# Feed-forward weight sums: two of the four by adding transfers, two on GpSimd, lower block row negated

## The reference, cut to what matters

```
def _swiglu(x, w_gate, w_up, w_down):
    return (jax.nn.silu(x @ w_gate) * (x @ w_up)) @ w_down
```

## Time and profile before

| | us |
|---|---|
| median of 3 runs | 2102.5 (2102.32 to 2103.25) |
| span of the profiled execution | 2102.9 |
| PE busy | 2066.9, 98% of the span |
| DVE busy | 1351.0, 64% |
| ACT busy | 1013.6, 48% |
| POOL busy | 722.4, 34% |

### The profile page before, as it was taken

One profiled execution on the slowest core, in us unless ns is written; L12 is line 12 of the kernel. 1 busy time (PEld: TensorE's weight loads), 2 busy tenths in 40 slices (PEclk: granted clock), 3 DMA queues, 4 the chain that ended last, 5 costly groups with the idle time before them and its releaser, 6 DMA issues.

```text
span 2102.9 us, 31133 instructions
## 1 busy us (share of the span) xinstructions
PE 2066.9 (98%) x10658; PEld 1753.4 (83%) x10658; DVE 1351.0 (64%) x2278; ACT 1013.6 (48%) x1788; POOL 722.4 (34%) x544
## 2 busy tenths in 40 slices
PE   8999999999999999999999999999999999999998
PEld 6778888888988888988887788888878888888886
DVE  6497863667752366674277889899767337676523
ACT  4466663533433353434344577767655325344322
POOL 2133452513233163442337511211165315233331
PEclk9999999999999999999999999999999999999999
DMA  5333263334433244443335322222364534445331
GB/s 175 96 103 103 76 225 100 119 117 155 140 123 97 80 130 130 150 149 110 91 94 171 100 71 89 73 80 86 118 203 131 178 97 126 135 132 167 100 99 61
DMA packets 74383, 251.31 MB, mean 120 GB/s; under 512 B 8264, under 2 KB 8520, under 8 KB 73776
## 3 DMA queue, kind: packets, MB, share of 16 engines
q1 hardware_dynamic: 51120, 182.08, 28.2%
q0 software_dynamic: 11456, 40.72, 5.8%
q10 hardware_dynamic: 11712, 27.27, 3.5%
HBM read 229.57 MB, written 18.89 MB: 118 GB/s over the span
## 4 chain that ended last, share of the span: by engine, by line
PE 87%; DVE 8%; ACT 2%; issue 2%; DMA 1%; DVEq 0%; SPq 0%; ACTq 0%
PE bank L188 25%; PE bank L190 25%; PE bank L189 25%; PE bank L195 3%; PE bank L194 3%; PE bank L2166 1%; DVE w_lo L162 1%; DMA w_raw<-stream 1%; PE bank L2833 1%; PE bank L920 1%; PE bank L2835 1%; PE bank L347 1%; PE bank L349 1%; PE bank L354 1%; PE bank L2841 1%
## 5 line engine op out<-in xcount | busy, mean ns | idle before, releaser
L162 DVE TENSOR_TENSOR w_lo<-w_raw,w_hi 128x1024 fp32r<-128x1024 f32 x337 | 454.0, 1350 | 410.2 <-ACT w_hi L157 407.0
L188 PE MATMUL bank<-xn_hi,w_hi 128*128 128x512 f32 (+1 forms) x1432 | 554.5, 387 | 6.1 <-DVE w_lo L162 4.2
L157 ACT ACTIVATE w_hi<-w_raw 128x1024 fp32r<-128x1024 f32 x337 | 354.7, 1055 | 417.7 <-PE bank L190 249.6
L189 PE MATMUL bank<-xn_lo,w_hi 128*128 128x512 f32 (+1 forms) x1432 | 538.6, 376 | 0.0
L190 PE MATMUL bank<-xn_hi,w_lo 128*128 128x512 f32 (+1 forms) x1432 | 538.5, 376 | 0.0
L188 PEld LDWEIGHTS bank<-xn_hi,w_hi 128*128 128x128 f32 x1432 | 270.2, 189 | 58.0 <-DVE h L622 6.0
L190 PEld LDWEIGHTS bank<-xn_hi,w_lo 128*128 128x128 f32 x1432 | 269.5, 188 | 50.1
L189 PEld LDWEIGHTS bank<-xn_lo,w_hi 128*128 128x128 f32 x1432 | 270.3, 189 | 44.6 <-issue 2.6
L188 PE MATMUL bank<-down_hi,w_hi 128*128 128x512 f32 x528 | 205.8, 390 | 0.0
L190 PE MATMUL bank<-down_hi,w_lo 128*128 128x512 f32 x528 | 205.4, 389 | 0.0
L189 PE MATMUL bank<-down_lo,w_hi 128*128 128x512 f32 x528 | 205.4, 389 | 0.0
(11 more groups left out here) (473 smaller groups left out, 4228.1 us busy)
## 6 DMA issues: line engine op xcount, KB each, us to landing
w_raw<-stream SPq DMA_DIRECT2D x337, 512.0 KB, 3.6
s_raw<-stream POOLq DMA_DIRECT2D x48, 512.0 KB, 6.4
spill_g<-gate_out ACTq DMA_DIRECT2D x16, 256.0 KB, 2.0
m_more<-spill_g POOLq DMA_DIRECT2D x3, 1024.0 KB, 13.2
x<-xt SPq DMA_DIRECT2D x4, 512.0 KB, 6.9
x<-xt ACTq DMA_DIRECT2D x1, 2048.0 KB, 11.5
spill_x<-x ACTq DMA_DIRECT2D x1, 2048.0 KB, 7.6
spill_ga<-ga_out ACTq DMA_DIRECT2D x8, 256.0 KB, 3.3
```

The lines of the kernel that those rows point to most:

```text
L157: nc.scalar.activation(w_hi[:, slot, :], w_raw[:, slot % 2, :], ACT.Copy).then_inc(split_hi, 1)
L162: nc.vector.tensor_tensor(w_lo[:, slot, :], w_raw[:, slot % 2, :], w_hi[:, slot, :], ALU.subtract).then_inc(split_lo, 1)
L188: nc.tensor.matmul(to, a_hi, b_hi, start=start, stop=False, skip_group_check=True)
L189: nc.tensor.matmul(to, a_hi, b_lo, start=False, stop=False, skip_group_check=True)
```

## The change

The lower block row (up) enters the form with its sign turned, so that all four weight sums become additions. S1 and S3 are then made by transfers from DRAM that add into `s_raw` as they land: the first half of the up chunk is added to a22, and the first half of the gate chunk to a21. Both are issued by POOL once the two plain loads have landed, and POOL waits for both of them before it makes S2 and S4 as before. ACT waits for S1 and S3 on the transfers' own semaphores and for S2 and S4 on the count of POOL's sums. The turned sign is taken back in T1, T2 and T4 (a factor of -1 in ACT's `t_high` and DVE's `t_low`) and in the `gated` of the first tile; for this `gated` and `t_low` become scalar_tensor_tensor in place of tensor_tensor, all of them. POOL's loop over bodies is written out in Python, and `square_added`, which only f1 has, gets one more wait on its own last sum.

```
-            for k, n in (("sum", 4), ("hi", 4), ("lo", 4), ("gate", KT), ("gated", 0)):
-                merges[k] += n + 4 * BODIES
+                merges[k] += n + (2 if k == "sum" else 4) * BODIES
...
-                gates_n[g] += 16 * BODIES
+                gates_n[g] += 32 * BODIES
+            def landed(i, g, n):
+                return 32 * i + (gates_loaded[g] - 32 * FIRST_BODY + 16 * n)
...
-                    nc.scalar.activation(t_hi[:, n], t_raw[:, n], ACT.Copy).then_inc(c["hi"], 1)
+                    nc.scalar.activation(t_hi[:, n], t_raw[:, n], ACT.Identity, scale=T_SIGN[n]).then_inc(c["hi"], 1)
...
                 def s_high(n, i):
-                    act.wait_ge(c["sum"], summed(i))
+                    if n in (S1, S3):
+                        act.wait_ge(gates_in[0 if n == S1 else 1], landed(i, 0 if n == S1 else 1, 2))
+                    else:
+                        act.wait_ge(c["sum"], summed(i, 1 if n == S2 else 2))
...
-                    nc.vector.tensor_tensor(to, silu[t][:], to, ALU.mult).then_inc(s["product"], 1)
+                    nc.vector.scalar_tensor_tensor(to, silu[t][:], sign, to, ALU.mult, ALU.mult).then_inc(s["product"], 1)
...
                 def sums(i):
-                    for g in range(2):
-                        pool.wait_ge(gates_in[g], 16 * i + (gates_loaded[g] + 16 * (1 - FIRST_BODY)))
                     a11, a12, a21, a22 = (s_raw[:, g, half, :] for g in range(2) for half in range(2))
-                    nc.gpsimd.tensor_tensor(a22, a21, a22, ALU.add).then_inc(c["sum"], 1)
-                    nc.gpsimd.tensor_tensor(a21, a11, a21, ALU.subtract).then_inc(c["sum"], 1)
-                    pool.wait_ge(c["sum"], summed(i, 2))
-                    nc.gpsimd.tensor_tensor(a11, a22, a11, ALU.subtract).then_inc(c["sum"], 1)
-                    pool.wait_ge(c["sum"], summed(i, 3))
-                    nc.gpsimd.tensor_tensor(a12, a12, a11, ALU.subtract).then_inc(c["sum"], 1)
+                    gate_11, up_21 = (stream[4 * i + (first_in + g)][:, 0:HT * P] for g in range(2))
+                    pool.wait_ge(gates_in[0], landed(i, 0, 1))
+                    pool.wait_ge(gates_in[1], landed(i, 1, 1))
+                    pool.dma_start(a22, up_21, accum_op=ALU.add).then_inc(gates_in[0], 16)
+                    pool.dma_start(a21, gate_11, accum_op=ALU.add).then_inc(gates_in[1], 16)
+                    pool.wait_ge(gates_in[0], landed(i, 0, 2))
+                    pool.wait_ge(gates_in[1], landed(i, 1, 2))
+                    nc.gpsimd.tensor_tensor(a11, a22, a11, ALU.add).then_inc(c["sum"], 1)
+                    pool.wait_ge(c["sum"], summed(i, 1))
+                    nc.gpsimd.tensor_tensor(a12, a12, a11, ALU.add).then_inc(c["sum"], 1)
```

More of the change, by code:

```diff
@@ L279, in build_program @@
         S_AT = ((0, 0), (1, 1), (1, 0), (0, 1))
+        T_SIGN = (-1.0, 1.0, -1.0, -1.0)
         assert BODIES == KT
@@ L298, in feed_forward, with summed @@
             for g in range(2):
-                gates_n[g] += 16 * BODIES
-            def summed(i, n=4):
-                return 4 * i + (c0["sum"] + 4 - 4 * FIRST_BODY + n)
+                gates_n[g] += 32 * BODIES
+            def landed(i, g, n):
+                return 32 * i + (gates_loaded[g] - 32 * FIRST_BODY + 16 * n)
+            def summed(i, n):
+                return 2 * i + (c0["sum"] + 4 - 2 * FIRST_BODY + n)
             def part_made(k, i, n):
@@ L617, in normed, with gated @@
                     nc.vector.tensor_tensor(to, banks[bank][:], norm_r[:], ALU.mult).then_inc(s["scaled"], 1)
-                def gated(to, t, scaled, silus):
+                def gated(to, t, scaled, silus, sign=1.0):
                     dve.wait_ge(s["scaled"], scaled)
                     dve.wait_ge(s["silu"], silus)
-                    nc.vector.tensor_tensor(to, silu[t][:], to, ALU.mult).then_inc(s["product"], 1)
+                    nc.vector.scalar_tensor_tensor(to, silu[t][:], sign, to, ALU.mult, ALU.mult).then_inc(s["product"], 1)
                 def t_low(n):
                     dve.wait_ge(c["hi"], c0["hi"] + n + 1)
-                    nc.vector.tensor_tensor(t_lo[:, n], t_raw[:, n], t_hi[:, n], ALU.subtract).then_inc(c["lo"], 1)
+                    nc.vector.scalar_tensor_tensor(t_lo[:, n], t_raw[:, n], T_SIGN[n], t_hi[:, n], ALU.mult, ALU.subtract
+                                                   ).then_inc(c["lo"], 1)
                 def s_low(n, i):
@@ L675, in dve_part @@
                     nc.vector.tensor_tensor(h_tile(i, 0), h_tile(i, 0), norm_r[:], ALU.mult).then_inc(s["scaled"], 1)
-                    gated(h_tile(i, 0), 0, 4 * i + (2 * b + 3), 2 * i + (b + 2))
+                    gated(h_tile(i, 0), 0, 4 * i + (2 * b + 3), 2 * i + (b + 2), -1.0)
                     finished(dve, first_in, 3, i, N_IN)
@@ L764, in square_added @@
                     nc.gpsimd.tensor_tensor(fin_r[:], fin_r[:], joint_sq[:], ALU.add).then_inc(f["added"], 1)
+                    pool.wait_ge(f["added"], n + 1)
                 pool.wait_ge(c["gate"], c0["gate"] + KT)
@@ L780, in pool_part @@
                     nc.gpsimd.tensor_tensor(fin_r[:], x[:, 0, :], x[:, 0, :], ALU.mult).then_inc(f["added"], 1)
-                    with pool.Fori(FIRST_BODY, FIRST_BODY + KT - 1) as i:
+                    for i in range(FIRST_BODY, FIRST_BODY + KT - 1):
                         next_raw(i)
@@ L785, in pool_part @@
                 else:
-                    with pool.Fori(FIRST_BODY, FT // 2 - 1) as i:
+                    for i in range(FIRST_BODY, FT // 2 - 1):
                         next_raw(i)
```

## The result

The changed kernel takes 2114.9 us (median of 4 runs, 2113.4 to 2115.8), before 2102.9: a ratio of 1.005, interval 1.0038 to 1.0062. It is slower by 8 to 13 us. The profiled execution has a span of 2111.2 against 2102.9. A run's time is 2.0 to 2.6 us over its span wherever both are known. So the profiled execution of after, 2113.4, is the fastest of its four, and that of before, whose time is not known, would have taken about 2105, more than any of its four. The two traces therefore show 8.3 of the 12 us. It also means that the span before should not have been held against the median, as the table of times before does with "within 0.4 us" and the prediction's sum with its 0.4.

A forecast was written before the change was run, and what follows sets the result against it. PE, busy 98% of the 2102.9 us span, was taken as the bound. 2102.9 - 4.2 (removed sums) + 3.9 (`w_lo` stalls) + 0.1 (sign) = 2102.7, or 2102.3 against the median; range 2098.0 to 2118.0.

The forecast's parts named there:

- the loop of `s_raw` closes: Rival, 0.20: the single buffer's chain from issue to issue outlasts a body, from L = 7.3; 2124 at the upper bound.
- loads, issue to landed: First stretch of the `s_raw` chain, the plain loads' landing: 5.8 or 7.9 us, read from two bodies.
- L: Time from the first adding transfer's issue until both have landed: 5.5 us taken, bounds 4.6 to 8.6.
- ACT and DVE up to the next issue: End of the `s_raw` chain: two pairs of `s_hi` and `s_lo`, a copy and a `w_lo`, some 4 us.
- u: Time in us within a body, counted from its first matmul on PE.
- The ceiling: Most that could be gained: 4.2 us (0.20%) that PE loses in 21 bodies against 21.02 us each.
- The removed part: Two of POOL's four sums gone and the sums' place freed beside DVE's chain to L622: -4.2 us.
- POOL's loop written out: Loop over bodies unrolled on POOL; said to fall in POOL's idle time of 4.6 us or more: 0.
- The stall at S2 past s = 3.7: ACT's first `s_hi` waits for POOL's first sum; s up to 3.7 is covered, never reached with L = 5.5: 0.
- s: Start of POOL's first sum in us, counted from the start of the body using it; forecast -0.9 to +1.3.
- The window of s from 0 to 1.1 for `w_lo`: POOL's sums delay DVE's `w_lo` of chunk 2, stalling PE by s in a third of 21 bodies: +3.9 us.
- Sign, longer forms, extra wait: scalar_tensor_tensor on L622 +0.1 us; `t_hi` and `t_lo` in the plain tiles 0; the extra wait of `square_added` 0.

The follow-up runs named there:

- the hold: Kernel with the up chunk first, POOL's two sums of a body also held until DVE has made `w_lo` of chunk 2: 2100.3 us, ratio 0.9982.
- the up chunk first: Changed kernel, but the up chunk is loaded first and both adds are issued when it alone has landed: 2103.6 us, ratio 0.9996.
- the run without adds: Changed kernel with the two adding transfers and their waits left out, nothing in their place: 2101.4 us, ratio 0.9985.

## Why the prediction was wrong

The forecast was no change, 2102.3; the kernel is slower by 12 us, through the mechanism that the prediction has as "the loop of `s_raw` closes", with a chance of 0.20. The measured 2114.9 lies inside the stated range of 2098.0 to 2118.0, but only because that range took in part of this rival. The step that failed is the length of that chain, which was put under a body and is over it: forecast 13.8 + 5.5 = 19.3 us against a body of 21.1, measured 21.9 on average against 21.02. By its terms (medians over the turns inside the loops):

| from issue to issue, us | predicted | measured |
|---|---|---|
| loads, issue to landed | 5.8 or 7.9, mean 6.85 | 8.7 (8.1 to 9.2) |
| L, the adds | 5.5 | 6.4 (5.7 to 6.6; 6.7 to 7.1 in the first turns) |
| two sums | 2.9 | 2.66 |
| ACT and DVE up to the next issue | some 4 | 4.12 |

*The landing of the loads is the step that was off by the most,* 1.9 of the 2.6 us. The two turns that it was read from happen to include nearly the shortest one: over the 21 turns of the trace before, the landing is 5.7 to 8.6, median 7.6, which was there to be read. With the loop written out they are issued 0.4 us earlier and take longer, 8.2 (median of the kernel before with its loop written out). In the changed kernel the first loads inside each loop, at u = 8.6, took 8.7 to 8.9, and the later ones, at 9.6 to 11.8 in the closed chain, 8.1 to 9.2; why they took longer was not tested. With the measured terms the chain closes from L = 5.5 on, not from 7.3, so the L that was forecast would already have stood at the edge, while the measured L of 6.4 in a chain of 13.8 + L would not have closed it.

*L = 5.5 is the second.* It "counted them as copies of 512 KB" and then chose from the low end because the engines are quiet at that time. Measured is 5.7 to 7.1, inside the bounds of 4.6 to 8.6. The quiet did not help: the stretch of the adds shows the engines at 68% for 106 GB/s (the last two columns; the stretch of the copies stands at 37% for 124).

```profile
501.70:508.10 6.40, 6.40 (x47) 6.04 (x46) 2.52 (x3) 0.38 (x1) 1.75 (x2) 1.00 0.68 106
```

Twice the engine time of a copy was the right guess for the movement. Left out was POOL's own issue, 1.8 us for the two together in place of 1.1; the prediction names this as a sign of being wrong. The estimate from the Trainium skill (DMA: Bandwidth & Descriptors, Anatomy of one DMA), 3.8 us, was further off, and this case's runs disagree with it for plain copies too: 4.3 us for two of 256 KB, where by the same reading it gives some 3.2 as an estimate.

*The size of the loss* follows from the chain: 0.85 us a turn over 18 turns, less the 3.3 us of room that the first turns had. The prediction's 26 us took 1.3 a turn, for L at its upper bound, over 20 bodies, and gave no room.

*The ceiling* was right: 4.2 us lost in the bodies before, none with the hold. *The removed part,* -4.2 for two sums less, was wrong in its cause. PE's waits for L622 are gone, and L630 alone takes 0.69, but with POOL's loop written out and all four sums still there the bodies lose only 1.4 and 0.9 us. *POOL's loop written out* was put at 0 and is worth 3 of the 4.2 in these traces (2 us in the medians), which leaves about 1 for the removed sums.

*The stall at S2 past s = 3.7* was sized rightly (3.73), only with the remark that "with L = 5.5 it never gets there".

*The window of s from 0 to 1.1 for `w_lo`* (+3.9) is not met in the changed kernel, whose s is 2.0 or more inside the loops. As a mechanism it is real and was worked out exactly: with the up chunk first a body grows by s, as "a stall of s" says, up to 1.1 and not beyond.

*Sign, longer forms, extra wait*: 0 and +0.1 were right as far as the runs can tell; they were tested together and not one by one.

## What to carry to other kernels

A buffer that is filled, worked on in place and given back has a chain of its own, whatever engines its steps run on. Add up that chain from issue to issue and compare it with the period of the bound engine, before counting what work an engine is rid of. Take the landing times over all turns and not from one or two, and expect them to change when the transfers are issued at another point of the period. Where the chain is near the period, look who uses its results first: here another order of two uses, or an earlier start of half of the chain, was worth as much as the whole loss. In a short loop a chain that is a little too long costs only what exceeds the room of its first turns, so a remedy that adds room can hide that it is still too long.

An operation moved to another place on GpSimd takes turns with VectorE there too, if VectorE then works on two operands in SBUF. Here a sum delayed PE when it lay beside the last operations of a body or, by up to 1.1 us, beside the first ones of the next, and a wait that held it until DVE had made `w_lo` was better than starting it as early as possible.

## What the runs showed of the hardware

- A transfer of 256 KB that adds into SBUF took 0.88 us (the first of a pair) and 1.22 us (the second) at issue on GpSimd where a copy takes 0.54, landed after 5.2 us where a copy took 3.5, and kept the 16 DMA engines busy for 4.1% of the span (48 adds, 6912 packets) against 1.9% (48 copies, 3840 packets).
- The loads of `s_raw` landed no earlier when they were issued earlier: issued at u = 8.6 to 8.7 they had landed at 16.7 to 17.5 in the run without adds, issued at 9.0 to 9.1 at 14.7 to 17.7 before (by the start of POOL's first sum).
- POOL's sum of 128x512 and DVE's work on two SBUF operands took turns: `w_lo` took 2.31 us in place of 1.22 and the gated line 1.74 in place of 0.69 where a sum lay beside them.
- In a loop on GpSimd with register counts, the issue of the first load came at u = 9.0, 0.4 us later than with the loop written out (8.6).
